# Block 2's head loop: weight splits moved behind the softmax steps of heads 8 to 12, and neighbours laid apart

## The reference

```
h = rms_norm_2(x, attn_pre_norm)
mix = hybrid_mixer_2(h, ...)        # fox, nsa and dilated attention, then @ w_out
x = x + rms_norm_2(mix, attn_post_norm)
x = x + rms_norm_2(conv_ffn(rms_norm_2(x, ffn_pre_norm), ...), ffn_post_norm)
```

## Time and profile before

| | before |
|---|---|
| median of three executions | 2106.05 us (2103.40 to 2112.19) |
| the profiled execution | 2109.53 us |
| its span, first to last instruction | 2107.7 us |
| mean granted TensorE clock | 0.977 of full |
| PE busy | 2003.4 us, 95% of the span |
| PE weight loads busy | 1901.6 us, 90% |
| DVE busy | 1406.4 us, 67% |
| ACT busy | 1160.2 us, 55% |
| POOL busy | 142.3 us, 7% |

### The profile page before, as it was taken

The page is one execution under the profiler, slowest core; times in us unless marked ns, Lnnn a source line. Parts: engine busy times, 40 slices in busy tenths (PEclk is TensorE's granted clock), DMA queues, the critical chain, the costliest instruction groups (busy, mean ns, idle before and its releaser), DMA issues.

```text
span 2107.7 us, 39543 instructions
## 1 busy us (share of the span) xinstructions
PE 2003.4 (95%) x15240; PEld 1901.6 (90%) x15240; DVE 1406.4 (67%) x2072; ACT 1160.2 (55%) x1847; POOL 142.3 (7%) x153
## 2 busy tenths in 40 slices
PE   7999989989999999989989999998999999898998
PEld 7999969989999999978989999976899998678997
DVE  5765887666655665788656656775588568738973
ACT  5444666554445444576455445575666457656753
POOL 1062100010000000100000001000100010002000
PEclk9999999999999999999999999998999999999999
DMA  5545433445545545443445545441245544304543
GB/s 213 206 169 185 150 125 125 151 170 184 185 156 194 198 158 186 167 151 105 153 163 181 193 149 183 162 160 41 81 164 197 173 154 152 137 3 156 202 163 116
DMA packets 53533, 329.80 MB, mean 156 GB/s; under 512 B 5936, under 2 KB 6704, under 8 KB 27952
## 3 DMA queue, kind: packets, MB, share of 16 engines
q1 hardware_dynamic: 53424, 328.34, 44.5%
HBM read 327.27 MB, written 1.05 MB: 156 GB/s over the span
## 4 chain that ended last, share of the span: by engine, by line
PE 61%; DVE 13%; issue 8%; ACT 6%; DVEq 5%; DMA 4%; POOLq 3%; POOL 1%; ACTq 0%; SPq 0%
PE bank L657 16%; PE bank L658 16%; PE bank L659 16%; DVE w_lo L636 5%; DMA raw<-in_w 4%; PE bank L704 3%; ACT w_hi L597 2%; DVE conv L1362 1%; PE bank L669 1%; PE bank L1651 1%; PE bank L671 1%; PE bank L1635 1%; DVEq L1356 1%; PE bank L1652 1%; PE bank L1653 1%
## 5 line engine op out<-in xcount | busy, mean ns | idle before, releaser
L636 DVE TENSOR_TENSOR w_lo<-raw,w_hi 128x2048 fp32r<-128x2048 f32 (+3 forms) x348 | 673.6, 1939 | 343.5 <-ACT w_hi L597 316.2
L657 PE MATMUL bank<-h_hi,w_hi 128*128 128x256 f32 x2704 | 779.2, 288 | 8.4 <-DVE conv L2024 3.4
L658 PE MATMUL bank<-h_lo,w_hi 128*128 128x256 f32 x2704 | 768.0, 284 | 0.0
L659 PE MATMUL bank<-h_hi,w_lo 128*128 128x256 f32 x2704 | 767.6, 284 | 0.0
L597 ACT ACTIVATE w_hi<-raw 128x2048 fp32r<-128x2048 f32 (+2 forms) x346 | 560.3, 1623 | 142.2 <-DMA raw<-in_w 118.6
L657 PEld LDWEIGHTS bank<-h_hi,w_hi 128*128 128x128 f32 x2704 | 522.0, 193 | 14.9 <-issue 8.5
L658 PEld LDWEIGHTS bank<-h_lo,w_hi 128*128 128x128 f32 x2704 | 522.1, 193 | 1.2
L659 PEld LDWEIGHTS bank<-h_hi,w_lo 128*128 128x128 f32 x2704 | 521.8, 193 | 0.0
L657 PE MATMUL bank<-hid_hi,w_hi 128*128 128x256 f32 x1056 | 295.4, 280 | 0.0
L658 PE MATMUL bank<-hid_lo,w_hi 128*128 128x256 f32 x1056 | 295.4, 280 | 0.0
L659 PE MATMUL bank<-hid_hi,w_lo 128*128 128x256 f32 x1056 | 295.3, 280 | 0.0
(11 more groups left out here) (339 smaller groups left out, 2960.5 us busy)
## 6 DMA issues: line engine op xcount, KB each, us to landing
raw<-in_w SPq DMA_DIRECT2D x198, 1024.0 KB, 4.8
raw<-in_w SPq DMA_DIRECT2D x96, 704.0 KB, 4.1
raw<-in_w SPq DMA_DIRECT2D x52, 768.0 KB, 4.2
raw<-in_w SPq DMA_DIRECT2D x8, 512.0 KB, 3.5
raw<-in_w SPq DMA_DIRECT2D x4, 576.0 KB, 3.7
x<-in_x SPq DMA_DIRECT2D x1, 1024.0 KB, 5.0
out<-x SPq DMA_DIRECT2D x4, 256.0 KB, 2.4
const<-in_const SPq DMA_DIRECT2D x1, 548.0 KB, 5.7
```

The source lines that it names most:

```text
L636: dve.tensor_tensor(w_lo[:, s % SPLIT_SLOTS, 0:n], raw[:, s % RAW_SLOTS, 0:n], w_hi[:, s % SPLIT_SLOTS, 0:n].bitcast(F32), ALU.subtract).t ...
L657: pe.matmul(out, hi, x_hi, start=start, stop=False, skip_group_check=skip)
L658: pe.matmul(out, hi, x_lo, start=False, stop=False, skip_group_check=skip)
L659: return pe.matmul(out, lo, x_hi, start=False, stop=stop, skip_group_check=skip)
```

## The change

Three things are changed, all in block 2's head loop.

1. ACT and DVE no longer split the next weight at `cmp0`, `ca1`, `cmp1`, `f6` and `f7` (`SPLIT_BESIDE`). Units 15 to 19 are split in rounds 8 to 12, one in each: on ACT behind the exponentials of head n and the normalization of head n-1, on DVE behind the maxima of head n and the inverse sums of head n-1 (`SPLIT_BEHIND`). Unit 20 is split on ACT behind head 14's exponentials, on DVE behind head 16's maxima (it was 14).
2. On ACT the value copy of round n stands ahead of the exponentials of head n, for n over 3 (the `EVAC2` loop).
3. `ct` moves from round 9 to round 10, `cum1` from 13 to 15, and `R7` from 14 to 17.

```diff
-               5: [...], 7: [("ca", 0), ("cmp", 0)], 8: [("ca", 1), ("cmp", 1)], 9: [("ct", 0)],
...
+               10: [("ct", 0), ("f", 6), ("c2", 0)], 11: [("cum", 0)], 12: [("SC", 0), ("f", 7)], 13: [("R", 6)],
...
+SPLIT_BEHIND = {8: ("f", 6), 9: ("f", 7), 10: ("O", 0), 11: ("O", 1), 12: ("O", 2)}
+SPLIT_BESIDE = [("cmp", 0), ("ca", 1), ("cmp", 1), ("f", 6), ("f", 7)]
...
 for n in range(3, len(HEADS2)):
-    at = EVAC2.index(("S", n))
-    EVAC2[at], EVAC2[at + 1] = EVAC2[at + 1], EVAC2[at]
+    step = EVAC2.index(("S", n))
+    EVAC2.remove(("S", n))
+    EVAC2.insert(step + (1 if n == 3 else 2), ("S", n))
...
-            last = UNIT_OF2["O", 3] if n > 12 else max(due_)
+            last = max(due_)
...
-                if g in UNIT_OF2 and kind != "O" and g != ("vb", 1):
+                if g in UNIT_OF2 and kind != "O" and g != ("vb", 1) and g not in SPLIT_BESIDE:
                     split.until(at2 + UNIT_OF2[g] + AHEAD)
...
                 elif kind == "S":
-                    split.until(freed_by_scores(at2, i))
+                    if i < 8:
+                        split.until(freed_by_scores(at2, i))
                     softmax_act_exp(act, probs2, row2, i % PROBS2, max2_ready(l, i + 1), exp2_ready)
                     for n in due(i, len(HEADS2)):
                         softmax_act_norm(act, probs2, row2, n % PROBS2, sums2_ready(l, n + 1), probs2_ready)
+                    if i in SPLIT_BEHIND:
+                        split.until(at2 + UNIT_OF2[SPLIT_BEHIND[i]])
+                    if i == 14:
+                        split.until(at2 + UNIT_OF2["O", 3])
...
-                if g in UNIT_OF2 and kind != "O" and g not in (("vb", 1), ("f", 0)):
+                if g in UNIT_OF2 and kind != "O" and g not in (("vb", 1), ("f", 0)) and g not in SPLIT_BESIDE:
                     split.until(at2 + UNIT_OF2[g] + AHEAD)
...
-                    if i == 14:
+                    if i in SPLIT_BEHIND:
+                        split.until(at2 + UNIT_OF2[SPLIT_BEHIND[i]])
+                    if i == 16:
                         split.until(at2 + UNIT_OF2["O", 3])
```

## The result

| | before | after |
|---|---|---|
| median of nine executions each | 2106.24 us (2103.40 to 2112.19) | 2117.25 us (2114.29 to 2120.47) |
| ratio | | 1.005, 95% interval 1.0039 to 1.0062 |
| the profiled execution | 2109.53 us | 2114.29 us |
| its span | 2107.7 us | 2112.5 us |
| mean granted TensorE clock | 0.977 | 0.975 |

The kernel became slower by 11.0 us in the medians, 0.5%, where 3.5 were forecast.

The account below looks back on a forecast made before the run. PE was taken to bound the kernel before, the ring on ACT and DVE after. Layer 0 +0.2 less 0.4 and layer 1 +4.1 less 0.4 made +3.5 us together: 2113.0 profiled, 2110 against the median, range 2098 to 2121.

Parts of the forecast that it names:

- the ring: Rounds 8 to 12: maxima wait for `w_lo`, this for `w_hi`, this for exponentials, those for maxima; 7.1 us a head.
- the wait at `c2`: Layer 0: PE idle from 1409.3 until `h_rep` comes behind two splits, a new wait of 5.7 us; start about 1415.1.
- rival A: The clock falls a second time in each layer, between 1438 and 1457: +12.5 us, 2118.5 us; chance 0.20.
- Two old waits go: PE's waits at `ct` and at head 12's values, about 4.5 us each in each layer, go with their low-clock stretches.
- if the low clock lasted 3 us behind `c2` instead of 9: Error check behind `c2`: with the shorter low clock the chain moves by 1 us, as PE is not its bound.
- PE's forecast waits of 0.8, 0.7, 2.0 and 2.3 us: PE's short waits: 0.8 for `TC`, 0.7 before head 15, 2.0 and 2.3 before the transposes of heads 12 and 13.
- I take no fall: The short waits late in the loop were taken not to lower the clock, PE being busy over half the stretch.
- The profiled one stood 3.5 us above the median of the three, so against the median it is 2109.6: Profiled execution 2109.53 us plus 3.5 makes 2113.0; its 3.5 us above the median taken off gives 2109.6, rounded 2110.
- Layer 1 was better off before: Layer 1 had shorter low stretches, head 18 at 1853.52; the new chain gives 1857.6: +4.1 us, and 0.4 back.
- Rival B: The ring does not bind behind `c2`: -8 us in layer 0, -4 in layer 1, 2094 us; chance 0.12.
- rival C: No new wait: 18 us of waits and 13 or more of low clock go, 2075 us; chance 0.04.
- the three signs that would prove the forecast wrong: `c2` starts before 1412, PE idles less than 8 us a layer in this loop, or the clock is low twice there.

Follow-up runs that it names:

- experiment 4: The changed kernel with round 10's split put behind `ct`'s copy on ACT and behind `h_rep` on DVE: 2110.02 us, 1.0017 of before.
- experiment 6: The changed kernel with ACT's halves of the splits ahead of the exponentials as before, DVE's still behind the maxima: 2098.34 us, 0.9964 of before.
- experiment 11: The kernel before with the table's moves, value copies first, and on ACT unit 16's split behind the second gelu: 2107.75 us, 0.9997 of before.
- experiment 12: As experiment 11, with DVE's half of unit 16's split also behind head 9's maxima: 2087.30 us, 0.9904 of before.

## Why the prediction was right, and where its size was off

The path and the waits were right: the ring, its turn, the wait at `c2`, the times of what follows. The size was not: +3.5 us were forecast, +11.0 measured. The median of 2117.25 us stands 7 us above the forecast of 2110 and lies in the range because the range took in rival A, whose 2118.5 it comes near by luck: half of the miss is another term.

- **"Two old waits go", "a new wait of 5.7 us at `c2`", at "about 1415.1".** Right: 5.82 us in both layers, at 1414.39. Counted from T0 this is 51.5 us, where 51.0 were forecast.
- **The ring, 7.1 us a head, "takes their place".** Right, and shown by cutting it (19 us). Counted from T0, T13 came 0.8 us later than forecast, V12 and `K0` 1.1 to 1.2 (V12 at 1449.03, `K0` at 1456.47 after a wait of 1.06), head 18's scores about 0.8 (1459.50).
- **"if the low clock lasted 3 us behind `c2` instead of 9".** The 9 us were too few, it was 20. It cost little, as this sentence went on that PE is not the bound there: in the trace of after the steps of the ring and of the compressed softmax, from head 11's exponentials at 1420.26 to the last `w_hi` ahead of T13 at 1445.60, wait for PE once, 0.26 us, and experiment 4 has the ring's steps at the same times with the clock up and down. PE's forecast waits of 0.8, 0.7, 2.0 and 2.3 us were used up by PE's slowness: the trace of after shows 1.0 and less there in layer 0.
- **"I take no fall".** Wrong, and this was rival A in a smaller size. All four traced loops of the changed kernel have a second low stretch at T13. What the clock takes in it, length times the share that is missing, is 1.7 us (6 us at 0.72) and 3.4 (8 us at 0.57) in the first trace, 4.9 and 4.8 in the second. T13 to T18 took 24.8 us in the mean of four, and 22.9 in experiment 6, where the clock stays up there. This term is worth 1.8 us a layer, some 3.7 in both. The Trainium skill's rule on it ("TensorE: Matmul & The Clock Gate", "A second HAM failure mode: psum-queue depth-cycling"), which the prediction gave, is borne out only in part: the clock did fall in this stretch, though at less than rival A's 4.5 us a layer, but it fell at the wait for T13 (or the one next to it), the first or second of the short ones, and not after several in a row, and it was back at `K0`. What brings it down is not shown: experiment 6 has waits of 1.33 and 1.06 us there and keeps 1.00.
- **The baseline.** "The profiled one stood 3.5 us above the median of the three, so against the median it is 2109.6." The excess of 3.5 us was carried over to the changed kernel and then taken off. But it sat in the very stretch that the change replaces: V12's wait had 10.9 us of low clock behind it in that execution and 3 to 4 us in the three other traced loops of this kernel, and the second trace's loop of layer 0 takes 3.5 us less. The changed kernel has no such wait, and nothing could be taken off. "Layer 1 was better off before" was the typical layer, not the exception.

The sum with these: loops of before 208.5 us by its second trace, of after 219.4 in the mean of two, +10.9, where the medians have 11.0. The forecast +3.5, and 3.7 for the baseline, and 3.7 for the second stretch make 10.9. That this closes to a tenth is luck, as the two traces of after differ by 1.8 us. By milestones a layer: -6.2 from T0 to T7, where `ct` no longer waits; +13.0 from T7 to T13, by the ring and `h_rep`; -1.3 from T13 to T18.

Rival B (the ring doesn't bind) and rival C (no new wait) fell. Of the three signs that would prove the forecast wrong, the last came, the clock low twice in a loop.

## What to carry to other kernels

Two engines that hand work to each other in two ways (maximum to exponentials, `w_hi` to `w_lo`) form a ring when each puts one way behind the other; putting ScalarE's halves ahead again was worth 19 us here. Before converting a sum from a profiled execution to the median, ask where that execution's excess lies: if in the part that is changed, it does not carry over. The same holds for what an experiment gains: the trace of the ring cut was 5 us better than its kernel's median. And where a stretch is suspected of being bound by a chain and not by an engine's clock, look at two layers in which the clock falls at different places, and compare when the chain's own steps come, counted from the same milestone.

## What the runs showed of the hardware that was not expected

- A stretch at 1.2 GHz can last long after TensorE is busy again. Behind `c2` PE was busy without a gap for 16 to 20 us at 0.50: behind waits of 5.82, 3.72, 1.98, 1.45 and 0.84 us alike (the last in layer 1 of experiment 11). Behind the waits at `ct` before, on other work, it ended after 7 to 9 us. What ends it is open.
- The same wait at the same place can leave the clock up or bring it down: 1.98 us in both layers of experiment 4, low behind it in one only; 1.29 us at `J0` in both layers of experiment 12, low in layer 0 only; 1.07 and 1.23 us at `c2` left it up in experiment 6. V12's wait of 4.46 us in the kernel before had 10.9 us of low clock behind it in one loop and 3 to 4 in three. This may also be what spreads the executions of a kernel whose `c2` waits a little (2092.4 to 2105.5 us in experiment 6): the mean granted clock is 0.981 to 0.984 in its three fastest and 0.980 and 0.978 in its two slowest, but only one has a trace. What decides it is open.
- Where PE was the bound, one such stretch cost 8 us (43.0 against 35.1); beneath the ring it cost nothing that the milestones show (43.4 and 43.6).
